# Summing the modulation's partial results over the partitions: one-column fp32 matmuls in place of transposes and a reduction

## The chip, the core and the metric

The kernel runs on one core of one Trainium2 chip. The metric is the device time in microseconds. Engines are named as in the profile: PE is TensorE's matmuls, PEld its weight loads, DVE is VectorE, ACT ScalarE, POOL GpSimd, SP the queue that issues the DMAs. A record is one instruction as the profiler saw it.

## What is computed

Two transformer blocks on 256 positions of 1024 features, one after the other. The first is modulated: a vector c gives shifts, scales and gates for its norms and residuals, and these come from one large product of a single row with a matrix.

```python
c_act = jax.nn.silu(c)                               # 1 x 1024
mod = c_act @ w_ada[l] + b_ada[l]                    # 1024 x 6144
sh1, sc1, g1, sh2, sc2, g2 = jnp.split(mod, N_MOD, axis=-1)
h = modulate(rms_norm(x, norm1_w[l]), sh1, sc1)      # h * (1 + scale) + shift
mix = hybrid_mixer(h, ...)                           # gated delta rule + short convolution
x = x + g1[:, None, :] * mix
h = modulate(rms_norm(x, norm2_w[l]), sh2, sc2)
x = x + g2[:, None, :] * swiglu(h, w_ffn_in[l], w_ffn_out[l])
shf, scf = jnp.split(c_act @ w_ada_f + b_ada_f, 2, axis=-1)   # 1024 x 2048
return modulate(rms_norm(x, normf_w), shf, scf)
```

The second block (attention with a relative bias, and a gated feed-forward part with a convolution) takes no modulation.

## The kernel before

All activations lie transposed, features on the partitions and the 256 positions along the free axis. Weights stream through three raw buffers of 128 x 2048 fp32 (1 MB a transfer). Each half of a raw buffer is a unit: ACT copies it to a rounded fp32r half (`wh`, L1454), DVE takes the rest (`wl`, L1841), and PE multiplies in three products: high weights by high activations, low by high (both L1093), high by low (L1099). Five pairs of `wh`/`wl` go round. The whole program is one list of events, `plan`, written by a simulated schedule in Python: a product's tile calls `tick()`, which moves every waiting task one step. Each engine then goes through `plan` in its order and issues its own part of each event; semaphores tie them together. So the order on every engine is fixed when the program is built.

The modulation's matrix, `ada`, has 16 blocks of 512 output columns, each in two transfers (kp 0 and 1). For a block, DVE multiplies 8 slices of 128 rows by the matching column of silu(c) and adds them in `accs` (128 x 512; `dve_ada`, L1737 and L1740). Each partition then holds a partial sum of all 512 columns, and these are still to be summed over the 128 partitions and laid out as 4 columns of 128 in `modc`. That is `ada_reduce` (L481): it waits six ticks (`LATER`), takes one of the two `misc` PSUM banks, lets PE work (event "red", 0: L1252), and two ticks later lets DVE work (event "red", 1: `dve_reduce`, L1746). Block 0 and the first half of block 1 go another way: PE multiplies the raw rows itself (L1232), ACT copies the resulting row (L1474), and four matmuls turn it into columns (L1241), to which DVE adds the bias (L1869). Block 1's own partial sum is added onto that.

What depends on it: `accs` has two buffers, and the next user waits for PE's "red"; a `misc` bank is free again after DVE's "red"; `mod_scale` (L1821), the scales of the norm and the residuals wait for "mod". Blocks 2, 3 and 1 are reduced in start-up, before and between the norm's first scales; their last use leads to the first product. Sixteen matmuls of `ones` by `eye` (L1249) stand before block 3's group and ten (L1084) before the first product; their results are not used. Blocks 8 and 9, 4 and 5, 6 and 7 come with the products gb, z and scout, and 10 to 15 with the first feed-forward part.

Of the kernel before, what the change touches and what calls it, by code (L numbers as in the profile page):

```python
# [8 lines left out]
ALU = mybir.AluOpType  # L9
# [167 lines left out]
MM = dict(stop=True, skip_group_check=True)  # L177
# [7 lines left out]
def _program(nc, a, out, ctx):  # L185
    def sb(name, shape, dt=F32, where=ctx):
        return where.enter_context(nc.sbuf_tensor(name, shape, dt))

    def signal(name, step=1):
# [12 lines left out]
    v_lo, v_ev, v_misc, v_gdn, v_att, v_norm = (signal("dve_" + n) for n in ("lo", "ev", "misc", "gdn", "att", "norm"))  # L202
# [4 lines left out]
    psum = [ctx.enter_context(nc.psum_tensor(f"ps{i}", [128, 512], F32)) for i in range(BANKS)]  # L207
# [10 lines left out]
    w1c = sb("w1c", [128, 8])  # L218
    w1n = sb("w1n", [128, 8])
    shn = sb("shn", [128, 8])  # L220
    adr = sb("adr", [128, 4])
    silc = sb("silc", [128, 8])
    R = sb("R", [128, T])
    accs = [sb(f"acc{i}", [128, 512]) for i in range(2)]
# [32 lines left out]
        bank=psum[8 - STREAMS + i]) for i in range(STREAMS)]  # L257
# [37 lines left out]
    eye = cst[:, CST["eye"]:CST["eye"] + 128]  # L295
    ones = cst[:, CST["ones"]:CST["ones"] + 128]
# [98 lines left out]
    def emit(*event):  # L395
        plan.append(event)
        made.add(event[0] if len(event) == 1 else event[0:3])
# [53 lines left out]
        while ("lo", u) not in made:  # L451
            low_before(cursor["lo"] + 1)

    rows_bank, reduced = [], []
    sums = {}

    def ada(i):
# [23 lines left out]
    def ada_reduce(b, slot):  # L481
        for _ in range(LATER):
            yield
        while b == 1 and ("turn", 1, 1) not in made:
            yield
        bank, before = yield from take(misc)
        emit("red", b, 0, slot, bank, before)
        acc.give(slot, p_misc, "red", b)
        yield
        yield  # L490
        emit("red", b, 1, slot, bank, reduced[-1] if reduced else None)
        reduced.append(b)
        misc.give(bank, v_misc, "red", b)

    def mod(b):
# [719 lines left out]
    def tensor_engine(e):  # L1215
        for ev in plan:
# [7 lines left out]
            elif kind == "ada_rows":  # L1224
                _, i, b, before = ev
# [4 lines left out]
                for n in range(4):  # L1230
                    kt = 4 * kp + n
                    ins = e.matmul(psum[b][0:1, :], silc[:, kt:kt + 1], raw[i % RAW][:, 512 * n:512 * n + 512],  # L1232
                                   start=kt == 0, **MM)
                ins.then_inc(*p_misc.up("rows", i))
            elif kind == "turn" and ev[2] == 1:
                _, blk, _, s, b, before = ev
                free(e, before)
                a_misc.wait_ge(e, "row", blk)
                d_cst.wait_ge(e, "cst")
                for n in range(4):  # L1240
                    ins = e.matmul(psum[b][:, n:n + 1], accs[s][0:1, 128 * n:128 * n + 128], ones[0:1, 0:1], start=True,  # L1241
                                   **MM)
                ins.then_inc(*p_misc.up("turn", blk))
            elif kind == "red" and ev[2] == 0:
                _, blk, _, s, b, before = ev
                free(e, before)
                if blk == 3:
                    for _ in range(16):
                        e.matmul(psum[b][:, 0:128], ones, eye, start=True, **MM)  # L1249
                v_misc.wait_ge(e, "ada", summed[blk][-1])  # L1250
                for n in range(4):
                    ins = e.transpose(psum[b][:, 128 * n:128 * n + 128], accs[s][:, 128 * n:128 * n + 128], eye)  # L1252
                ins.then_inc(*p_misc.up("red", blk))
            elif kind == "norm_sq":
                _, n, j, s, _, b, before = ev
                free(e, before)
                d_cst.wait_ge(e, "cst")
                a_norm.wait_ge(e, "sq", n, j)
                e.matmul(psum[b][:, 0:T], ones, sqs[s][:, 0:T], start=j == 0, **MM)
                e.matmul(psum[b][:, 0:T], ones, sqs[s][:, T:2 * T], start=False, **MM).then_inc(*p_norm.up("sq", n, j))  # L1260
            elif kind == "norm_col":
                b = ev[2]
                free(e, ev[3])
                a_norm.wait_ge(e, "r", N3)
                for t in range(2):
                    ins = e.matmul(psum[b][:, t:t + 1], R3[0:1, cs[t]], ones[0:1, 0:1], start=True, **MM)
                ins.then_inc(*p_norm.up("col"))
            elif kind == "norm_sum":
                _, n, s, b, before = ev
                free(e, before)  # L1270
                g_norm.wait_ge(e, "part", n, 3)
                e.matmul(psum[b][:, 0:T], ones, sqs[s][:, 0:T], start=True, **MM).then_inc(*p_norm.up("sum", n))
            elif kind == "close":
                _, n, _, s, _, s0, b, before, b2, before2 = ev
                free(e, before)
                g_norm.wait_ge(e, "part", n, 2)
                e.matmul(psum[b][:, 0:T], ones, sqs[s0][:, 0:T], start=True, **MM).then_inc(*p_norm.up("part", n))
                a_norm.wait_ge(e, "sq", n, 6)
                e.matmul(psum[b][:, 0:T], ones, sqs[s][:, 0:T], start=False, **MM)
                a_norm.wait_ge(e, "sq", n, 7)  # L1280
                e.matmul(psum[b][:, 0:T], ones, sqs[s][:, T:2 * T], start=False, **MM).then_inc(*p_norm.up("sum", n))
                warm(e, n, b2, before2)
            elif kind == "decays" and ev[1] == 3:
                b = ev[3]
                free(e, ev[4])
                v_misc.wait_ge(e, "G40")
                a_misc.wait_ge(e, "beta")
                for c in range(2):
                    e.transpose(psum[b][:, 64 * c:64 * c + 40], G40[0:40, cs[c]], eye[0:40, 0:40])
                e.matmul(psum[b][:, 128:136], G40[0:8, 127:128].to_broadcast([8, 128]), eye[0:8, 0:8], start=True,  # L1290
                         **MM).then_inc(*p_misc.up("G"))
            elif kind == "vturn":
                _, j, _, m, b, before = ev
                free(e, before)
                a_misc.wait_ge(e, "silu_v", j)
                for n in range(4):
                    ins = e.transpose(psum[b][:, 128 * n:128 * n + 128], tmps[m][:, 128 * n:128 * n + 128], eye)
                ins.then_inc(*p_misc.up("vturn", j))
            elif kind == "l2sum":
                _, j, n, s, b, before = ev  # L1300
                free(e, before)
                a_misc.wait_ge(e, "sq", j, n)
                e.matmul(psum[b][:, :], ones, sqs[s][:, :], start=True, **MM).then_inc(*p_misc.up("l2sum", j, n))  # L1303
            elif kind == "bias":
                b = ev[3]
                free(e, ev[4])
                d_dc.wait_ge(e, "dc")
                e.matmul(psum[b][0:16, 0:384], vec[0:32, VEC["rel"]:VEC["rel"] + 16], DC[:, 0:384], start=True,
                         **MM).then_inc(*p_misc.up("bias"))
# [433 lines left out]
            else:  # L1743
                ins.then_inc(*v_misc.up("ada", i))

    def dve_reduce(e, b, bank, previous):  # L1746
        col = modc[:, 4 * b:4 * b + 4]
        bias = col if b == 1 else v("b_ada", 4 * b, 4) if b < 12 else v("b_ada_f", 4 * (b - 12), 4)
        p_misc.wait_ge(e, "red", b)
        if previous is not None:  # L1750
            v_misc.wait_ge(e, "mod", previous)
        e.tensor_reduce(adr[:, :], psum[bank][:, :].rearrange("p (a b) -> p a b", a=4), mybir.AxisListType.X,
                        ALU.add).then_inc(*v_misc.up("red", b))
        v_misc.wait_ge(e, "red", b)
        if b == 1:
            v_misc.wait_ge(e, "turn", 1)
        e.tensor_tensor(col, adr[:, :], bias, ALU.add).then_inc(*v_misc.up("mod", b))

    def dve_scale(e, n, j, m, before):
        a_norm.wait_ge(e, "r", N2 if n == N3 else n)  # L1760
# [71 lines left out]
    def vector_engine(e):  # L1832
        for ev in plan:
            kind = ev[0]
            if kind == "lo":
                u = ev[1]
                un = units[u]
                i, n, c = un["item"]["i"], un["n"], un["c"]
# [26 lines left out]
            elif kind == "turn" and ev[2] == 1:  # L1865
                _, blk, _, s, b, _ = ev
                p_misc.wait_ge(e, "turn", blk)
                d_vec.wait_ge(e, "vec")
                ins = e.tensor_tensor(modc[:, 4 * blk:4 * blk + 4], psum[b][:, 0:4], v("b_ada", 4 * blk, 4), ALU.add)  # L1869
# [1 line left out]
                if blk == 0:  # L1871
                    v_misc.at[("turn", 0)] = v_misc.at[("mod", 0)]
            elif kind == "red" and ev[2] == 1:
                dve_reduce(e, ev[1], ev[4], ev[5])
            elif kind == "residual":
                _, n, j, pn = ev
                p = products[pn]
                b = psum[p["banks"][0]]
# [14 lines left out]
            elif kind == "close":  # L1893
                n, p = ev[1], products[ev[2]]
                for i in range(2):
                    kt, b = 6 + i, psum[p["banks"][i]]
# [9 lines left out]
            elif kind == "l2":  # L1906
                _, j, n, s = ev
# [3 lines left out]
            elif kind == "decays":  # L1911
                k = ev[1]
                if k == 0:
                    p = products[ev[3]]
# [16 lines left out]
                elif k == 4:  # L1931
                    b = psum[ev[3]]
# [17 lines left out]
            elif kind == "normed":  # L1950
                p = products[ev[1]]
# [9 lines left out]
            elif kind == "scx":  # L1961
                p, m = products[ev[1]], ev[3]
# [61 lines left out]
            elif kind == "bias":  # L2024
                b = ev[3]
# [153 lines left out]
```

## Time and profile before

| | |
|---|---|
| time, median of 3 runs | 913.32 us (912.99 to 917.46) |
| profiled execution | 921.88 us |
| its span, first to last instruction | 920.1 us |
| mean granted TensorE clock | 0.993 |
| instructions | 18632 |
| PE busy | 893.8 us (97%) |
| DVE busy | 667.6 us (73%) |
| ACT busy | 505.1 us (55%) |
| POOL busy | 65.8 us (7%) |

Busy time is the sum of an engine's records. Matmuls are pipelined, so the time that one occupies is read from the distance between the starts of successive records and not from its own duration, which is more than twice that. The chain that ended last is followed back from the last instruction, at each step to what released it.

### The profile page before, as it was taken

How to read it: one execution, taken by the hardware profiler on the slowest of the kernel's cores; microseconds unless marked ns; L12 is line 12 of the kernel's file. 1: busy time of each engine (PE TensorE's matmuls, PEld its weight loads, DVE VectorE, ACT ScalarE, POOL GpSimd, SP SyncE). 2: the span in 40 equal slices, each digit the busy share in tenths (PEclk: the TensorE clock that was granted, in tenths of full speed). 3: DMA queues.
4: the chain of work that ended last, by engine and by line, in shares of the span. 5: the costliest groups of instructions: out<-in, count | busy, mean ns of one | idle time of the engine just before them, and what ended most of it. 6: DMA issues, size and time to landing. Idle time of an engine off the chain costs nothing.

```text
span 920.1 us, 18632 instructions
## 1 busy us (share of the span) xinstructions
PE 893.8 (97%) x8020; PEld 850.1 (92%) x8020; DVE 667.6 (73%) x1132; ACT 505.1 (55%) x814; POOL 65.8 (7%) x83
## 2 busy tenths in 40 slices
PE   5998999999999999999999999999999999999997
PEld 2798998999898999999999999999899999999997
DVE  4878767566978677677798775588665688778652
ACT  2489667454354627555354444466665576666442
POOL 0100201021001001020000000120000200000011
PEclk9999999999999999999999999999999999999999
DMA  8754233333767665465988889526331455555631
GB/s 335 279 191 162 102 129 104 128 138 109 259 232 247 209 229 179 165 217 179 288 326 295 287 287 255 218 96 226 138 138 53 177 184 192 190 192 178 223 126 46
DMA packets 27681, 177.31 MB, mean 193 GB/s; under 512 B 2864, under 2 KB 5680, under 8 KB 7504
## 3 DMA queue, kind: packets, MB, share of 16 engines
q1 hardware_dynamic: 27600, 176.13, 54.7%
q8 instruction: 63, 1.03, 0.4%
q14 instruction: 18, 0.15, 0.0%
HBM read 174.29 MB, written 1.84 MB: 191 GB/s over the span
## 4 chain that ended last, share of the span: by engine, by line
PE 82%; DVE 8%; ACT 6%; DMA 2%; issue 1%; DVEq 0%; SPq 0%; ACTq 0%
PE ps L1093 46%; PE ps L1099 22%; PE ps L1091 2%; DVE wl L1841 2%; DVE acc L1740 1%; ACT wh L1454 1%; PE ps L1138 1%; PE ps L1146 1%; PE ps L1232 1%; PE ps L1149 1%; PE ps L1097 1%; DMA raw<-in_ada_dram 1%; PE ps L1252 1%; PE ps L1303 1%; DMA raw<-in_w_sc_dram 1%
## 5 line engine op out<-in xcount | busy, mean ns | idle before, releaser
L1093 PE MATMUL ps<-HH,wh 128*128 128x256 f32 x1480 | 374.1, 288 | 0.7 <-DVE wl L1841 0.2
L1841 DVE TENSOR_TENSOR wl<-raw,wh 128x1024 fp32r<-128x1024 f32 x265 | 320.2, 1228 | 73.4 <-ACT wh L1454 72.8
L1093 PE MATMUL ps<-HH,wl 128*128 128x256 f32 x1480 | 361.0, 279 | 0.0
L1454 ACT ACTIVATE wh<-raw 128x1024 fp32r<-128x1024 f32 x265 | 273.8, 1043 | 142.5 <-PE ps L1099 112.9
L1093 PEld LDWEIGHTS ps<-HH,wh 128*128 128x128 f32 x1480 | 280.4, 189 | 9.8 <-issue 4.3
L1093 PEld LDWEIGHTS ps<-HH,wl 128*128 128x128 f32 x1480 | 279.8, 189 | 1.9 <-issue 1.9
L1099 PE MATMUL ps<-HL,wh 128*128 128x256 f32 x1480 | 229.1, 279 | 0.3 <-DVE HL L1786 0.3
L1099 PEld LDWEIGHTS ps<-HL,wh 128*128 128x128 f32 x1480 | 197.1, 189 | 0.6 <-DVE HL L1786 0.5
L1093 PE MATMUL ps<-FH,wh 128*128 128x256 f32 x352 | 85.9, 278 | 0.0
L1093 PE MATMUL ps<-FH,wl 128*128 128x256 f32 x352 | 85.9, 278 | 0.0
L1740 DVE SCALAR_TENSOR_TENSOR acc<-raw,silc,acc 128x512 f32<-128x512 f32 x101 | 76.3, 756 | 8.0 <-DMA raw<-in_ada_dram 4.9
L1093 PEld LDWEIGHTS ps<-FH,wh 128*128 128x128 f32 x352 | 66.5, 189 | 0.0
L1093 PEld LDWEIGHTS ps<-FH,wl 128*128 128x128 f32 x352 | 66.3, 188 | 0.0
L1723 DVE SCALAR_TENSOR_TENSOR tmp<-ps,vec,tmp 128x255 f32<-128x255 f32 (+2 forms) x112 | 46.0, 474 | 27.5 <-ACT tmp L1522 25.8
L1099 PE MATMUL ps<-FL,wh 128*128 128x256 f32 x352 | 56.3, 279 | 0.0
L2073 POOL TENSOR_TENSOR sq<-sq 128x256 f32<-128x256 f32 x16 | 15.1, 943 | 515.4 <-ACT sq L1496 515.2
L1099 PEld LDWEIGHTS ps<-FL,wh 128*128 128x128 f32 x352 | 47.6, 188 | 0.0
L1613 ACT ACTIVATE FH<-tmp 128x512 fp32r<-128x512 f32 x22 | 14.0, 635 | 57.5 <-DVE tmp L2009 29.9
L1093 PE MATMUL ps<-YH,wh 128*128 128x256 f32 x128 | 32.6, 290 | 0.0
L1093 PE MATMUL ps<-YH,wl 128*128 128x256 f32 x128 | 31.3, 280 | 0.0
L1522 ACT ACTIVATE tmp<-ps,vec 128x256 f32<-128x256 f32 x44 | 22.3, 556 | 7.7 <-PE ps L1099 7.7
L1093 PEld LDWEIGHTS ps<-YH,wh 128*128 128x128 f32 x128 | 24.4, 191 | 0.5
(269 smaller groups left out, 1080.9 us busy)
## 6 DMA issues: line engine op xcount, KB each, us to landing
raw<-in_ada_dram SPq DMA_DIRECT2D x32, 1024.0 KB, 5.2
raw<-in_w_fi_dram SPq DMA_DIRECT2D x22, 1024.0 KB, 4.9
raw<-in_w_up_dram SPq DMA_DIRECT2D x22, 1024.0 KB, 4.8
raw<-in_w_rest_dram SPq DMA_DIRECT2D x20, 1024.0 KB, 4.8
raw<-in_w_in_dram SPq DMA_DIRECT2D x16, 1024.0 KB, 4.8
raw<-in_w_qkv_dram SPq DMA_DIRECT2D x12, 1024.0 KB, 4.8
raw<-in_w_o_dram SPq DMA_DIRECT2D x8, 1024.0 KB, 4.8
raw<-in_w_fo_dram SPq DMA_DIRECT2D x8, 1024.0 KB, 5.0
```

Of the source, the lines that this page charges most:

```text
L1091: e.matmul(o, x_hi[:, k0 + k, 128 * t:128 * t + 128], w[:, k, :], start=first and n + k == 0, **MM)
L1093: e.matmul(o, w[:, k, 128 * t:128 * t + 128], x_hi[:, k0 + k, :], start=first and n + k == 0, **MM)
L1097: ins = e.matmul(o, x_lo[:, k0 + k, 128 * t:128 * t + 128], wh[:, k, :], start=False, **MM)
L1099: ins = e.matmul(o, wh[:, k, 128 * t:128 * t + 128], x_lo[:, k0 + k, :], start=False, **MM)
L1138: ins = e.matmul(bank[g, 64 * c:64 * c + 64], S[f"d{n % 2}"][g, c, :], xz[g, 0, c, :], start=True, **MM)
L1454: e.activation(whl[u % HALF][0][:, 0:n], raw[i % RAW][:, c:c + n], ACT.Copy).then_inc(*a_hi.up(u))
L1522: e.activation(tmps[m][:, T * t:T * t + T], b[:, T * t:T * t + T], ACT.Identity, scale=v("conv2", 88 + ft), bias=v("conv2_b", ft)).then_in ...
L1613: e.activation(flat(dst, j), tmps[m][:, :], ACT.Copy).then_inc(*a_ev.up("hi", src, j))
L1723: e.scalar_tensor_tensor(out=cv, in0=b[:, T * t:T * t + T - s], scalar=tap, in1=cv, op0=ALU.mult, op1=ALU.add).then_inc(*v_ev.up("conv", n ...
L1740: ins = e.scalar_tensor_tensor(out=acc_, in0=w, scalar=c, in1=acc_, op0=ALU.mult, op1=ALU.add)
L1841: e.tensor_tensor(wl[:, 0:n], raw[i % RAW][:, c:c + n], wh[:, 0:n].bitcast(F32), ALU.subtract).then_inc(*v_lo.up(u))
L2073: e.tensor_tensor(sqs[s][:, 0:T], sqs[s][:, 0:T], sqs[s][:, T:2 * T], ALU.add).then_inc(*g_norm.up(*(("sum", n, j) if j else ("part", n, 0))))
```

## The change

The four transposes of a block's partial sums become four matmuls that have the same partial sums as weights and one column of ones as the streamed operand: each gives 128 sums over the partitions, in one column of PSUM. DVE then adds the bias straight from the four PSUM columns; the reduction and its small buffer `adr` go (a buffer of the same size keeps the layout of the memory). The plan, its order, the banks and the DMAs stay. "red" of DVE is now the same event as "mod".

```diff
@@ -218,7 +218,7 @@
-    adr = sb("adr", [128, 4])
+    sb("home_s", [128, 4])
@@ -488,8 +488,7 @@
-        emit("red", b, 1, slot, bank, reduced[-1] if reduced else None)
-        reduced.append(b)
+        emit("red", b, 1, slot, bank)
@@ -1249,7 +1248,7 @@
                 v_misc.wait_ge(e, "ada", summed[blk][-1])
                 for n in range(4):
-                    ins = e.transpose(psum[b][:, 128 * n:128 * n + 128], accs[s][:, 128 * n:128 * n + 128], eye)
+                    ins = e.matmul(psum[b][:, n:n + 1], accs[s][:, 128 * n:128 * n + 128], ones[:, 0:1], start=True, **MM)
                 ins.then_inc(*p_misc.up("red", blk))
@@ -1743,18 +1742,14 @@
-    def dve_reduce(e, b, bank, previous):
+    def dve_reduce(e, b, bank):
         col = modc[:, 4 * b:4 * b + 4]
         bias = col if b == 1 else v("b_ada", 4 * b, 4) if b < 12 else v("b_ada_f", 4 * (b - 12), 4)
         p_misc.wait_ge(e, "red", b)
-        if previous is not None:
-            v_misc.wait_ge(e, "mod", previous)
-        e.tensor_reduce(adr[:, :], psum[bank][:, :].rearrange("p (a b) -> p a b", a=4), mybir.AxisListType.X,
-                        ALU.add).then_inc(*v_misc.up("red", b))
-        v_misc.wait_ge(e, "red", b)
         if b == 1:
             v_misc.wait_ge(e, "turn", 1)
-        e.tensor_tensor(col, adr[:, :], bias, ALU.add).then_inc(*v_misc.up("mod", b))
+        e.tensor_tensor(col, psum[bank][:, 0:4], bias, ALU.add).then_inc(*v_misc.up("mod", b))
+        v_misc.at[("red", b)] = v_misc.at[("mod", b)]
```

## Rows read from the trace of the kernel before

**Rows 1.** The page's engine table: busy us, share, instructions.
```profile
PE 893.8 (97%) x8020; PEld 850.1 (92%) x8020; DVE 667.6 (73%) x1132; ACT 505.1 (55%) x814; POOL 65.8 (7%) x83
```

**Rows 2.** The page's chain that ended last, shares by engine.
```profile
PE 82%; DVE 8%; ACT 6%; DMA 2%; issue 1%; DVEq 0%; SPq 0%; ACTq 0%
```

**Rows 3.** Windows: stretch, length, PE, PEld, DVE, ACT, POOL, clock, DMA share, GB/s.
```profile
250.00:300.00 50.00, 48.25 (x494) 45.27 (x493) 41.30 (x74) 23.71 (x47) 5.96 (x10) 1.00 0.71 248
300.00:345.00 45.00, 43.67 (x464) 41.35 (x463) 32.61 (x54) 21.27 (x32) 1.45 (x3) 0.96 0.62 215
480.00:545.00 65.00, 65.00 (x570) 65.00 (x569) 54.38 (x67) 30.86 (x36) 0.00 (x0) 1.00 0.82 289
```

**Rows 4.** Windows of L1252 alone: PE and PEld records.
```profile
0.00:36.00 36.00, 1.97 (x12) 1.26 (x12) 1.00 0.86 324
236.00:545.00 309.00, 7.36 (x48) 5.40 (x48) 0.99 0.70 241
```

**Rows 5.** Line 1752 on DVE: ns min/median/max, first and last start.
```profile
L1752 DVE TENSOR_REDUCE adr<-ps x15: 673/683/690, 24.5 to 544.6; 128x4 f32<-128x512 f32 x15
```

**Rows 6.** Timeline (start, us, engine, line): a block in the product stream.
```profile
272.40 0.60 PE L1252 MATMUL ps<-cst,acc 128*128 128x128 f32 x4
...
272.96 0.28 PE L1093 MATMUL ps<-HH,wl 128*128 128x256 f32 x1
```

**Rows 7.** Timeline: two fp32 matmuls in the product stream.
```profile
340.72 0.39 PE L1174 MATMUL ps<-lc,inv 128*128 128x128 f32 x2
340.94 0.39 PE L1168 MATMUL ps<-v,k 128*128 128x128 f32 x2
...
341.28 0.28 PE L1093 MATMUL ps<-YH,wl 128*128 128x256 f32 x1
```

**Rows 8.** Timeline: runs of fp32 passes, 128- and 64-column weight tiles.
```profile
414.78 2.17 PE L1212 MATMUL ps<-cst 128*128 128x128 f32 x18
...
314.90 0.68 PE L1138 MATMUL ps<-xz,d 64*64 64x64 f32 x16
```

**Rows 9.** Timeline: four fp32 matmuls that stream one column.
```profile
33.39 1.05 PE L1241 MATMUL ps<-cst,acc 1*128 1x1 f32 x8 [0.68 <-ACT acc L1474]
```

**Rows 10.** Timeline of start-up: blocks 2, 3 and 1 and what follows.
```profile
22.69 0.59 ACT L1474 ACTIVATE acc<-ps 1x512 f32<-1x512 f32 x1 [1.90 <-PE ps L1252]
...
28.15 3.84 PE L1249 MATMUL ps<-cst 128*128 128x128 f32 x32
...
32.06 0.66 PE L1252 MATMUL ps<-cst,acc 128*128 128x128 f32 x4
...
32.75 0.59 ACT L1474 ACTIVATE acc<-ps 1x512 f32<-1x512 f32 x1 [3.96 <-PE ps L1252]
...
34.68 0.15 DVE L1869 TENSOR_TENSOR modc<-ps,vec 128x4 f32<-128x4 f32 x1
...
34.89 0.66 PE L1252 MATMUL ps<-cst,acc 128*128 128x128 f32 x4 [0.45 <-DVE modc L1869]
...
36.46 0.16 DVE L1757 TENSOR_TENSOR modc<-adr,modc 128x4 f32<-128x4 f32 x1
...
37.80 0.19 PEld L1093 LDWEIGHTS ps<-HH,wh 128*128 128x128 f32 x1 [0.22 <-DVE wl L1841]
...
42.48 0.50 PE L1099 MATMUL ps<-HL,wh 128*128 128x256 f32 x2 [0.34 <-DVE HL L1786]
```

**Rows 11.** The chain in order of time: start, us, what.
```profile
281.80 0.61 DVE adr L1752
```

**Rows 12.** Timeline of PE: three waits in the middle.
```profile
282.16 0.71 PE L1119 MATMUL ps<-KT 128*128 128x128 f32 x4 [1.58 <-ACT qg L1355]
...
297.74 0.45 PE L1146 MATMUL ps<-y,xz 64*64 64x64 f32 x8 [0.17 <-ACT y L1368]
...
322.49 0.44 PE L1155 MATMUL ps<-xz,l 64*64 64x64 f32 x4 [1.32 <-DVE inv L1662]
```

**Rows 13.** Windows, columns as in rows 3: a stretch of lower clock.
```profile
324.00:327.50 3.50, 3.50 (x29) 3.16 (x28) 3.15 (x7) 1.06 (x1) 0.00 (x0) 0.51 0.59 234
```

More of the change, by code:

```diff
@@ L452, in low_of @@
             low_before(cursor["lo"] + 1)
-    rows_bank, reduced = [], []
+    rows_bank = []
     sums = {}
@@ L1873, in vector_engine @@
             elif kind == "red" and ev[2] == 1:
-                dve_reduce(e, ev[1], ev[4], ev[5])
+                dve_reduce(e, ev[1], ev[4])
             elif kind == "residual":
```

## The prediction

> **What bounds the kernel now.** First the page's engine table: the chip's TensorE (PE) is busy for 97% of the span [rows 1]. Busy is not the same as bound, so next the chain that ended last: 82% of the span is PE work, 8% VectorE (DVE), 6% ScalarE (ACT) [rows 2]. Then the stages in which the modulation runs. Between 480 and 545 us PE is busy 65.00 of 65 us; between 250 and 300 and between 300 and 345 us it is busy 48.25 of 50 and 43.67 of 45 us [rows 3]. So whatever a block adds to PE's stream there moves everything behind it, and DVE, at 41.30 of 50 and 54.38 of 65 us, has room. The windows cut to the edited line say where its blocks are: 12 transposes (3 blocks) before 36 us and 48 (12 blocks) between 236 and 545 us [rows 4]. These two groups need two sums. The first 36 us are another regime: there PE, ACT and DVE wait on each other in a chain.
>
> **The change, part by part.** *Removed on DVE:* 15 reductions of median 0.683 us [rows 5]; the 15 adds of the bias stay. That is 15 x 0.683 = 10.2 us less work for an engine that is busy 73% [rows 1]. It is worth something only where the chain runs through DVE.
>
> *Replaced on PE, in the stream.* Four transposes stand as four records. In one block they start at 272.40, the next product's second matmul starts at 272.96: 0.56 us [rows 6]. (I read to the second matmul because the start of the first one after a change of kind is out of step.) The new form is an fp32 matmul, which this trace records as two passes, each with its own weight load: the four matmuls of L1241 are eight records [rows 9]. Two fp32 matmuls of 128 columns, four records, in the same position occupy 340.72 to 341.28, again 0.56 us [rows 7]. So a pass costs what a transpose costs, and there are now two passes per matmul.
>
> Does the single streamed column make a pass cheaper? Two rows give the bounds of a pass. With 128 streamed columns, 18 passes of L1212 take 2.17 us with a last record of 0.275 (its neighbours' median), so (2.17 - 0.275)/17 = 0.111 us each [rows 8]. With one streamed column, L1241's eight take 1.05 us with a last record of about 0.245, so (1.05 - 0.245)/7 = 0.115, with a slower first gap in it [rows 9]. These two differ by a factor of 128 in what is streamed and agree in price; what they share is a weight tile of 128 columns. L1241 loads only one partition of weights and the new matmul loads 128, but L1212 loads 128 partitions at the same price. I take 0.112 us. The bound from below is the pass with a 64-column tile, which has neither that width nor that stream: 16 passes in 0.68 us, (0.68 - 0.23)/15 = 0.030 us [rows 8]; it is the further one, since the new weight tile is the 128-column one.
>
> The block's price on PE: four passes more than now, 4 x 0.112 = +0.45 us. For the 12 blocks from 236 to 545 us: +5.4 us.
>
> What of it is hidden? PE has three waits in that stretch with room in them. At 282.16 us it waits 1.58 us for ACT's qg [rows 12]; but that wait follows a DVE and ACT sequence that PE itself started, so it moves as a whole. The same holds at 322.49 us, where PE waits 1.32 us for DVE [rows 12], at the end of a sequence of table loads and gates on ACT that starts from PE. At 297.74 us PE waits 0.17 us for ACT's y [rows 12], on a branch that hangs on a weight transfer; here the extra PE time does fill the wait: -0.2. The one reduction that the chain shows in this stretch, 0.61 us at 281.80 [rows 11], opens that same branch (it sits before the split of the weights and the release of a raw buffer). Without it the branch comes 0.6 us earlier, but PE's own queue is then later by three blocks' +1.3, so PE is what is late next, and the 0.6 us buys nothing beyond these 0.2. From 345 us on no wait of PE follows a reduction. Middle: 5.4 - 0.2 = +5.2 us.
>
> *Start-up.* Here I walk the rows [rows 10]. In all three blocks PE's group grows by 0.45 us, and somebody waits for each. (a) Block 2 at 22.0 us: ACT's copy of block 0's row needs the accumulator that this group frees, so that copy (22.69 us), its four row matmuls and DVE's add come 0.45 us later; then the reduction's 0.7 us is gone, so the first scale comes about 0.27 earlier. PE, however, is held by that add: its next row matmuls and the 16 warm-up matmuls of L1249 (28.15 us, 3.84 us long) are 0.45 later. (b) Block 3 starts 32.06 now; L1249 had ended its last pass about 0.2 us earlier than needed, so it starts at 32.28 and, with eight passes at the 1.05 us of L1241's eight, ends at 33.33 instead of 32.72. ACT's copy (32.75) moves by +0.6, the row matmuls from 33.39 to 34.00, DVE's add from 34.68 to 35.07. (c) Block 1 waits for that add: 34.89 becomes 35.28, its eight passes end at 36.33, and DVE's last add ends near 36.52 instead of 36.62. Two reductions (0.7 each) are gone and DVE waits in their place. Result for DVE: 0.1 us earlier. PE's warm-up behind block 1 ends 0.65 us later (0.39 + 0.45, less the 0.2 us that PE waited for DVE's weights at 37.80), but at 42.48 us PE waits 0.34 us for DVE, and the chain then goes over a weight transfer and ACT, where PE has room. I take -0.1 us; ends: -0.5 (if only DVE's side counts) and +0.65 (if only PE's).
>
> Added waits: none in number. DVE's add now waits straight for PE's group. In the stream the group is done long before (block at 272.40, reduction of it at 281.80), so nothing queues behind it. In (c) the split of the first weights (L1841) and the second scale queue behind it, which is counted. No DMA is moved and no engine queue is reordered. Bank and accumulator: the bank is released 0.7 us earlier by DVE, and PE releases the accumulator 0.45 us later; outside start-up the next user is far behind.
>
> Sum: +5.2 - 0.1 = **+5.1 us**. The profiled execution took 921.88 us (span 920.1 and 1.8 around it) and would take 927.0. It is 0.9% above the median of the timed runs, 913.32 us; I carry the same +5.1 us over, as the span runs nearly throughout at full clock (mean 0.993): **918.4 us**, +0.56%.
>
> A rule that speaks against this sum: the Trainium skill, "TensorE: Matmul & The Clock Gate", section "Back-to-back issue gap", gives an isolated matmul a gap that goes with the streamed columns and is some 25 ns for 1 to 64 of them. By it eight one-column passes would take 0.2 us instead of the transposes' 0.45, and each block would gain 0.25 us. L1241's 0.115 us per one-column pass disagrees; the same page warns that the figure leaves out the weight load.
>
> **Rivals.** *The single column is cheap (not slower).* Mechanism: a pass costs what it streams, and the weight load hides behind the neighbouring product. Price: the lower bound 0.030 per pass, so 8 x 0.030 = 0.24 against 0.45, -0.2 us per block, -2.5 in the stream; start-up then gives back its reductions on the chain, about -1.4 (two of 0.7), less the waits of (a) that vanish; together -4: about 909.5 us. It decides from the point where a pass falls below half a transpose, 0.055 us. Against it: the agreement of rows 8 and 9. For it: L1241 has never been seen between two products. Chance 0.06.
>
> *The middle absorbs it.* The six blocks between 250 and 345 us lie where the chain changes between PE, DVE and a transfer. If it is DVE and the transfer that hold PE there (the waits of rows 12), the six cost nothing and the reduction at 281.80 counts: 6 x 0.45 - 0.2 = 2.5 us less, +2.6: 915.9 us. For it: those waits, and DVE's 41.30 of 50 us. Against it: PE's queue between the waits is unbroken. Chance 0.15.
>
> *A second half-speed stretch.* From 324 to 327.5 us the granted clock is 0.51 (1.2 of 2.4 GHz), after PE had stood still before 322.49 us [rows 13, 12]; 3.5 us at half speed lose about 1.7. If the shifted waits (282.16, for one, is as long as that) bring one more such stretch: +6.8, 920.1 us. Chance 0.08.
>
> *Nothing changes in what is issued* is ruled out by the diff: the kind of matmul differs.
>
> **How the numbers follow.** Forecast 0.71 (918.4, on its own 917.3 to 919.6: start-up's ends and 0.1 us around the hidden part); absorbed 0.15 (915.9); another half-speed stretch 0.08 (920.1); cheap column 0.06 (909.5). The range leaves out the last and little else: low 914.8 (the absorbed case less 1 us of scatter of a median), high 921.0 (the clock case plus 1). A difference of 0.5%, about what a measurement of this kernel can tell from no change, is 4.6 us; the forecast is only 0.5 us beyond it. Of its 0.71 I put 0.49 above the bound and 0.22 below it, since the runs of before scatter from 912.99 to 917.46. Slower 0.49 + 0.08 = 0.57; same 0.22 + 0.15 + 0.03 = 0.40; faster 0.03.
>
> **What would show it.** Right: the new line has 120 records where L1252 had 60; eight of them, between two products, span about 1.0 us to the second matmul behind them (0.56 now); no reduction on DVE; busy time of DVE down by 10 us with the span up by 5; DVE's last start-up add near 36.5; PE's wait at 297.74 gone. Wrong: passes well below 0.11 us apart (cheap column), or PE's waits between 280 and 325 us shorter by the 2 us and more that the blocks added (absorbed), or a window of clock 0.5 that was not there.

## The result and the profile after

The changed kernel is slower, and by more than forecast.

| | before | changed |
|---|---|---|
| time, median of 4 runs each | 913.15 us (911.15 to 917.46) | 928.23 us (921.48 to 930.95) |
| ratio | | 1.0148, interval 1.0081 to 1.0215 |
| profiled execution, span | 921.88, 920.1 us | 929.71, 927.6 us |
| mean granted clock in it | 0.993 | 0.994 |

Twelve more runs in each of two later sets gave 1.0078 (1.0053 to 1.0104; median 920.38) and 1.0094 (1.0059 to 1.0129; median 924.33). The best estimate, from all 28 runs of the changed kernel, mean 923.6 us, and 137 of the kernel before, mean 915.2, is +8.4 us, give or take 1.6. Three slow executions of the kernel before (924.47, 1454.62 and 4934.83 us) are left out here and in every mean below. Single executions of either kernel scatter over 10 us, and where that comes from is a large part of what follows.

The engine table of the changed kernel, then its chain, answer to [rows 1] and [rows 2].

```profile
PE 902.8 (97%) x8080; PEld 858.6 (93%) x8080; DVE 657.9 (71%) x1117; ACT 504.9 (54%) x814; POOL 65.5 (7%) x83
...
PE 85%; DVE 6%; ACT 6%; DMA 2%; issue 1%; POOL 0%; SPq 0%; DVEq 0%; ACTq 0%
```

DVE has lost 9.7 us of work and the 15 reductions; PE has 60 records more. Of the chain that ended last, DVE's share fell from 8% to 6% and PE's rose from 82% to 85%: the chain has moved to PE.

The timeline of PE at the block that answers to [rows 6], then one among the feed-forward products.

```profile
273.49 0.95 PE L1251 MATMUL ps<-cst,acc 128*128 128x1 f32 x8
274.30 0.36 PE L1092 MATMUL ps<-HH,wh 128*128 128x256 f32 x1
274.50 0.28 PE L1092 MATMUL ps<-HH,wl 128*128 128x256 f32 x1
...
439.83 0.95 PE L1251 MATMUL ps<-cst,acc 128*128 128x1 f32 x8
440.64 0.36 PE L1092 MATMUL ps<-HH,wh 128*128 128x256 f32 x1
440.85 0.28 PE L1092 MATMUL ps<-HH,wl 128*128 128x256 f32 x1
```

A pass is one of the two records of an fp32 matmul. From the start of the eight passes to the second matmul behind them it is 1.01 us, where four transposes took 0.56: +0.45 us a block, as forecast. L1251's windows, against [rows 4], show the doubled records, and that all of them are in the same places:

```profile
0.00:40.00 40.00, 3.06 (x24) 2.91 (x24) 0.95 0.84 313
236.00:550.00 314.00, 11.70 (x96) 11.71 (x96) 1.00 0.68 237
```

**Where the 7.5 us between the two profiled spans lie.** I cut both traces at the first matmul of three products and take differences of their starts. Up to the first scout product (four stream blocks): +2.4 us, of which 4 x 0.45 = 1.8 are the blocks. From there to the first product with the feed-forward activations (eight blocks): +2.5, which is 8 x 0.45 = 3.6, less the half-clock stretch of [rows 13] that the changed execution did not have (1.7), plus 0.6. From there to attention, where nothing was changed at all: **+2.6**. Behind it 0. These two windows show 51 us of that third part, before and changed:

```profile
545.00:596.00 51.00, 51.00 (x452) 51.00 (x451) 28.36 (x30) 22.57 (x26) 5.69 (x5) 1.00 0.80 248
...
549.00:600.00 51.00, 51.00 (x436) 51.00 (x435) 27.29 (x29) 22.34 (x25) 5.71 (x5) 1.00 0.74 228
```

PE never waits in either, the clock is 1.00 in both, and the changed kernel gets 436 matmuls through where the other got 452. The starts of its products are 118 ns apart, those of the other 113. The page cannot show this: PE is busy 51.00 of 51 us both times.

**Start-up.** The chain in order of time (start, us, what), against [rows 10]:

```profile
26.10 4.96 PE ps L1231 x8
31.06 3.77 PE ps L1248 x32
34.83 0.80 PE ps L1251 x8
...
36.30 1.06 PE ps L1240 x8
...
37.60 1.07 PE ps L1251 x8
38.66 0.02 issue
38.69 0.16 DVE modc L1751
```

DVE's last add starts at 38.69, where the forecast let it end near 36.52. The eight row records of L1231 took 4.96 us; they took 3.59 before. The windows say why (columns as in [rows 3]):

```profile
25.50:28.80 3.30, 3.04 (x7) 0.72 (x7) 2.54 (x9) 1.84 (x5) 0.44 (x1) 0.50 0.94 380
29.00:39.00 10.00, 9.07 (x65) 7.16 (x64) 6.83 (x13) 3.09 (x5) 1.10 (x2) 1.00 0.76 269
39.20:42.40 3.20, 3.20 (x18) 3.20 (x17) 3.16 (x7) 1.76 (x5) 0.36 (x1) 0.50 0.43 182
```

The granted clock is 0.50 (1.2 of 2.4 GHz) in two stretches that ran at full clock before. From 26.1 us to block 1 the chain of start-up is now nearly all PE's: rows, warm-ups, block 3, rows turned, block 1. Before, it ran there over DVE's sums of the next blocks (L1740).

Little of this delay lasts, though. The first product (37.81 us before) starts 4.4 us later, the one at 88.1 us 2.1 later, and from the one at 113.0 us on 0.5 to 0.6. PE's waits before 88 us take up one part. The other is a half-clock stretch that both kernels have near 90 us, and that is 6.8 us long before and 3.4 us changed (windows, before and changed):

```profile
88.50:95.50 7.00, 7.00 (x31) 6.42 (x31) 6.62 (x17) 2.58 (x7) 0.94 (x2) 0.51 0.09 26
...
90.40:93.60 3.20, 3.20 (x15) 2.88 (x14) 2.67 (x8) 2.47 (x6) 0.94 (x2) 0.50 0.18 74
```

### The profile page after: what moved, and what is told of

The parts are those of the page before. It is cut to its first block, busy times and chain, and to the rows that moved or that the text cites. A ratio compares the mean times of both kernels' runs of the same rounds, so it can differ in the third digit from the quotient of the medians.

```text
span 927.6 us, 18740 instructions
## 1 busy us (share of the span) xinstructions
PE 902.8 (97%) x8080; PEld 858.6 (93%) x8080; DVE 657.9 (71%) x1117; ACT 504.9 (54%) x814; POOL 65.5 (7%) x83
## 4 chain that ended last, share of the span: by engine, by line
PE 85%; DVE 6%; ACT 6%; DMA 2%; issue 1%; POOL 0%; SPq 0%; DVEq 0%; ACTq 0%
PE ps L1092 46%; PE ps L1098 22%; PE ps L1090 2%; PE ps L1231 2%; DVE wl L1836 1%; PE ps L1251 1%; ACT wh L1453 1%; PE ps L1137 1%; PE ps L1145 1%; PE ps L1148 1%; PE ps L1096 1%; DMA raw<-in_ada_dram 1%; PE ps L1302 1%; DVE acc L1739 1%; DVE KT L1722 1%
## 5 line engine op out<-in xcount | busy, mean ns | idle before, releaser
L1655 DVE TENSOR_TENSOR xz<-xz,ps 128x256 f32<-128x256 f32 x32 | 13.0, 417 | 17.9 <-PE ps L1148 17.6
```

The costliest lines, as they stand in the source:

```text
L1655: e.tensor_tensor(xz4, xz4, b[:, 0:T], ALU.subtract).then_inc(*v_gdn.up("xz", h, n))
```

## The experiments

The theory after the first profile (A): the passes cost 5.4 us; the rest is the spacing that the product stream falls into behind a block, and something of start-up. The spacing is the distance between the starts of two matmuls that follow each other in a product. The rival (B): start-up, now a chain on PE with half-clock stretches, is the whole excess.

**start_only**

```diff
-  ins = e.transpose(psum[b][:, 128 * n:128 * n + 128], accs[s][:, 128 * n:128 * n + 128], eye)
+  if blk < 4:
+      ins = e.matmul(psum[b][:, n:n + 1], accs[s][:, 128 * n:128 * n + 128], ones[:, 0:1], start=True, **MM)
+  else:
+      ins = e.transpose(psum[b][:, 128 * n:128 * n + 128], accs[s][:, 128 * n:128 * n + 128], eye)
```

(and the bias added straight from PSUM for the same blocks)

> Only blocks 2, 3 and 1, the three of start-up, take the one-column fp32 matmuls; the twelve in the product stream keep transposes and reduction. Theory A (what a block costs in the product stream, plus the spacing that the stream of products settles into behind each block, 113 or 118 ns a matmul): within 2 us of before. Theory B (start-up: in the changed kernel the last start-up block came 2.6 us later, with a granted clock of 0.5 from 25.5 to 28.9 us, and that delay is the excess over the forecast): slower by 5 us or more.

Measured 1.0019 (0.9994 to 1.0043); median 917.95 against 914.76. Against both theories as written, the 12 times fall into two groups: five of 912.2 to 914.0 with mean granted clocks of 0.994 to 0.998, and seven of 917.7 to 920.7 with 0.989 to 0.992. The mean is +1.7 us. So start-up is not the whole excess (B); that it is not nothing this run alone does not show, as the interval holds 1. Its profiled execution, of 914.04 us, has one stretch of half clock in start-up and yet stands beside the five shorter times, so one such stretch does not make the longer ones:

```profile
37.30:40.50 3.20, 3.20 (x17) 3.20 (x16) 3.16 (x8) 2.49 (x7) 1.12 (x1) 0.50 0.34 141
```

**stream_only** (the same edit with `blk > 3`)

> Only the twelve blocks in the product stream are changed. Theory A: as the changed kernel, +8 to +15 us, of which 5.4 are the passes and the rest more time at the 118 ns spacing. Theory B: +5 us, the passes alone. Theory C (passes alone count, and the spacing is drawn anew by each execution with no bias): +5 us in the mean, scattering by some 5.

Measured 1.0064 (1.004 to 1.0087): median 920.63, mean 920.95 against 914.84 of the kernel before on that chip, +6.1 us. All eight runs lie between 919.3 and 923.8, mean clocks 0.993 to 1.0. Below A's +8 and a little above the +5 of B and C: the passes and perhaps a little more (the interval is 3.7 to 8.0 us).

**twice** (the kernel before, its reductions kept)

```diff
+  if blk > 3:
+      for n in range(4):
+          e.transpose(psum[b][:, 128 * n:128 * n + 128], accs[s][:, 128 * n:128 * n + 128], eye)
   for n in range(4):
       ins = e.transpose(psum[b][:, 128 * n:128 * n + 128], accs[s][:, 128 * n:128 * n + 128], eye)
```

> The kernel before with the four transposes of each of the twelve stream blocks issued twice: the same +0.45 us of PE per block as the change, the reductions kept, no fp32 passes in these blocks. If only PE's time per block counts: +5.4 us. If the kind of matmul (fp32 passes against transposes) decides into which spacing the products fall: +5.4 with a share of the 118 ns spacing as before (0.52), while stream_only has more (0.63 in the changed kernel).

Measured 1.0041 (1.0023 to 1.0058), mean +4.0 us, where +5.4 was expected. PE's time per block is indeed nearly the same as the change's, 0.99 to 1.00 us to the second matmul behind the group (its timeline of PE; the first matmul after the group starts out of step):

```profile
437.54 0.60 PE L1253 MATMUL ps<-cst,acc 128*128 128x128 f32 x4
437.98 0.60 PE L1255 MATMUL ps<-cst,acc 128*128 128x128 f32 x4
438.34 0.37 PE L1093 MATMUL ps<-HH,wh 128*128 128x256 f32 x1
```

With the reductions kept it is 2 us cheaper than stream_only without them. So taking 12 reductions off DVE bought nothing that shows in the stream, and eight passes are, if anything, worse neighbours than eight transposes.

**after_again**

> The changed kernel once more, on the same chip as the others. Theory A: equal to stream_only within 2 us. Theory B: above stream_only by 5 or more. Its profile shows whether the spacing behind each block is the same as in the first one (fixed by the code) or drawn anew.

Measured 1.0078 (1.0053 to 1.0104), 0.8 us above stream_only by the mean: A rather than B. In this profile the 60 us behind the last block run at 113 ns and the last 200 too, unlike in the first one: the spacing is not fixed by the code.

**before_again** (the kernel before against itself)

> The kernel before against itself: no difference, and a second profile of it. Every theory expects 0 within 2 us. What is asked is which spacing (113 or 118 ns a matmul) its long last products fall into, and how often it has half-clock stretches before 90 us: if as often as start_only, the start-up change has no part in the two groups of times that start_only shows (912 to 914 and 918 to 921).

Measured 0.999 (0.9958 to 1.0022). Its profiled execution, the one of 1454.62 us, had a mean granted clock of 0.56, so the second profile that was wanted was still missing.

**start_warm** (start_only, with three unused matmuls before each of the groups that turn a row into columns)

```diff
+  for _ in range(3):
+      e.matmul(psum[b][:, 0:128], ones, eye, start=True, **MM)
   a_misc.wait_ge(e, "row", blk)
```

> start_only plus three unused 128-column fp32 matmuls on PE before each of the two row-turning groups, where PE waits for ACT anyway (0.67 us of passes each into waits of 0.9). Theory A (start-up has become so thin in streamed work that PE's clock is halved for a stretch in about half of the executions, +6 us): the slow group of times goes or gets rarer; median 912.5 to 914, 1 to 2 us below before. Theory B (the slow group comes from later delays of the chain): stays as start_only, two groups, median near 918.

Measured 1.001 (0.998 to 1.004), mean +1.5 us over the kernel before; the median, 916.28, lies between the two expected. Five of 12 runs have a mean clock of 0.993 or less, and the profiled one has a half-clock stretch in start-up still, from 38.5 us. Filling these waits did not remove it. The five, at 917.3 us in the mean, are hardly slower than the other seven, at 916.9.

**start_wide** (against start_only)

```diff
-  ins = e.matmul(psum[b][:, n:n + 1], accs[s][:, 128 * n:128 * n + 128], ones[:, 0:1], start=True, **MM)
+  ins = e.matmul(psum[b][:, 128 * n:128 * n + 128], accs[s][:, 128 * n:128 * n + 128], ones, start=True, **MM)
```

> start_only with 128 streamed columns of ones in place of one, in the three start-up blocks: as many passes at the same 0.112 us, the same sums in every column, DVE takes one of each 128. If the single column, which leaves the array idle in most of a pass, brings the half-clock stretches: the slow group goes, median 912.5 to 914. If the longer group and the shifted waits bring them: as start_only, half of the executions at 918 to 921.

Measured 1.0028 (0.9995 to 1.0061), mean +2.4 us; three of 12 at a clock of 0.993 or less. Neither run supports its idea of what brings the half-clock stretches; with 12 runs each, 7, 5 and 3 of 12 can't be told apart. Its profiled execution is one of the long ones, 921.09 us, and has no half-clock stretch before 88 us; it is long by its last 200 us, which took 7 us more than start_only's.

**stream_half** (it leaves out the sums of half of the columns)

```diff
-  for n in range(4):
+  for n in range(2 if blk > 3 else 4):
       if blk > 3:
-          ins = e.matmul(psum[b][:, n:n + 1], accs[s][:, 128 * n:128 * n + 128], ones[:, 0:1], start=True, **MM)
+          ins = e.matmul(psum[b][:, 2 * n:2 * n + 2], accs[s][:, 128 * n:128 * n + 128], ones[:, 0:2], start=True, **MM)
```

> stream_only with two of a block's four fp32 matmuls, each streaming two columns: four passes per block, as many as the transposes of before; the sums of half of the columns are left out, and their places get copies. If the number of passes is the price: within 1.5 us of before (-5.5 against stream_only). If a change of kind in the stream costs by itself, or the spacing behind an fp32 group is worse: +1 to +6 us remain. If DVE's removed reductions were worth something in the stream: below before.

Measured 1.0029 (1.0 to 1.0059), mean +3.5 us: outside the 1.5 us that the number of passes alone would give. The timeline of PE prices the block all the same, 0.56 us for four passes with two streamed columns:

```profile
436.77 0.50 PE L1253 MATMUL ps<-cst,acc 128*128 128x2 f32 x4
437.13 0.36 PE L1093 MATMUL ps<-HH,wh 128*128 128x256 f32 x1
437.33 0.28 PE L1093 MATMUL ps<-HH,wl 128*128 128x256 f32 x1
```

The block costs what it cost before, and yet the times are in two groups, 914.1 to 915.4 (four) and 920.3 to 923.0 (eight), ten of the twelve at clocks from 0.997 up. So there is a second two-valued thing beside the clock, of 6 us. The last 200 us show it, in the two profiles of the next runs.

**after_third and before_third** (the two kernels once more)

> The changed kernel once more, on another chip. Theory A (5.4 us of passes, plus 1 to 3 us of the slower spacing behind the one-column groups, start-up about nothing): +6 to +9 us in the ratio of the medians. If the +15 us of its first four runs is its true size: +12 or more.

> The kernel before against itself: 0 within 2 us, and an undisturbed second profile. Theory A: behind its transposes that are entered at the fast spacing (113 ns) about half stay fast; its last products (from 705 us) may run at 113 ns, against 118 in the first profile, which by itself makes 6 us of difference between two executions of one kernel.

Measured 1.0094 (1.0059 to 1.0129) and 1.0 (0.9964 to 1.0036). The second profile of the kernel before has a span of 911.1 where the first had 920.1. These are windows of the last products, first profile and second:

```profile
701.00:900.00 199.00, 198.21 (x1673) 196.81 (x1673) 143.99 (x210) 115.44 (x163) 10.23 (x10) 1.00 0.48 170
...
701.00:900.00 199.00, 198.94 (x1744) 197.53 (x1743) 143.74 (x209) 116.33 (x166) 11.21 (x10) 1.00 0.48 170
```

One kernel, full clock in both, 1673 and 1744 matmuls in 199 us. From the first matmul of the attention's output product to PE's last record the first took 220.8 us and the second 213.2: 7.6 of the 9 us between the spans. The 11 undisturbed profiles up to here all took either 213 to 214 or 220 to 221 us for this part.

Both new profiles have the 113 ns spacing there, so they are a fairer pair than the first: 919.6 against 911.1, +8.5 us. Of it 5.4 are the passes and 0.5 is left of start-up (where the changed kernel again has three half-clock stretches). Another 1.2 are a wait that the kernel before does not have, 3.4 us behind a block, for weights whose transfer came late:

```profile
467.14 0.35 PE L1092 MATMUL ps<-HH,wh 128*128 128x256 f32 x1 [0.94 <-DVE wl L1836]
```

after_again lost 0.9 us at the same matmul; in the first changed profile and in stream_only the wait is absent. Of the remaining 1.4 us of the pair 1.0 is spacing.

**probe_t and probe_8**

```diff
+  if first and part != "low" and p["kind"] in ("ug", "uv"):
+      for _ in range(4):
+          e.transpose(o[:, 0:128], eye, eye)                          # probe_t
+          e.matmul(o[:, 0:1], eye, ones[:, 0:1], start=True, **MM)    # probe_8
```

> The kernel before with four unused transposes ahead of each of the 22 products of the last up-projection. Price by the group: 22 x 0.45 = +9.9 us, and behind a group entered at the fast spacing about half stay fast, none stays slow: about a third of that stretch at 118 ns.

> The same with four unused one-column fp32 matmuls (eight passes) ahead of each of the 22 products. By the passes: 22 x 0.90 = +19.8 us, 9.9 above probe_t. Theory A on the spacing: every group turns fast into slow and slow into fast, so about half of the stretch runs at 118 ns, 1 us more. If a one-column pass were cheap (the rival of the prediction): +5 us or less.

Measured 1.0075 (1.0047 to 1.0102) and 1.0168 (1.0125 to 1.0211). Profile against before_third, for the same last part: 223.1 and 233.3 us against 213.2, so +9.9 and +20.1, which is 0.45 and 0.91 per group. The price per pass stands, and the rival of the cheap column (at most +5) is out. In the medians the distance to the kernel before is smaller (+7.6, +16.6). Likely that is because the kernel before sometimes falls into the 118 ns spacing there, and the probes' two profiles did so for only a few products: of the groups in their profiles that were entered at 113 ns, all but one were left at 113, after transposes and after one-column passes alike. So the expectation that each eight-pass group flips the spacing failed in this place.

**Four kernels with a quiet end.** Two of the probe's groups in the last up-projection, in the kernel before and three changed ones:

```diff
+  if first and part != "low" and p["kind"] == "ug" and p["j"] in (1, 2):
+      for _ in range(4):
+          e.transpose(o[:, 0:128], eye, eye)
```

> The kernel before with four unused transposes ahead of each of two products (ug 1 and 2) of the last up-projection, +0.9 us of PE. If such a group puts the products behind it back to 113 ns: the times above 917 us go, the median is 912.5 to 914.5 and the scatter is halved; it would then be faster than the kernel before by 0 to 2 us in the mean. If it does not: +0.9 us and the same two groups of times.

> start_only with the same two groups. Against tail_before: -0.1 by the forecast; +1.5 to +2 if half-clock stretches of start-up come in a larger share of its executions (mean granted clock 0.993 or less in about 5 of 12, 1 of 10 in tail_before).

> stream_only with the same two groups. Against tail_before: +5.2 by the forecast; +6 with 0.5 to 1 us of slower spacing behind the eight-pass groups before 610 us. Mean granted clock 0.993 or less in about 1 of 10.

> The changed kernel with the same two groups. Against tail_before: +5.5 if only the passes count (the forecast), +7 to +8.5 if start-up costs 1.5 to 2 and the spacing in the first feed-forward part 0.5 to 1. If the first four runs of the changed kernel (+15) were typical: +12 or more.

| kernel | runs | median, us | mean | mean less tail_before | clock 0.993 or less |
|---|---|---|---|---|---|
| tail_before | 12 | 914.62 | 915.2 | | 1 |
| tail_start | 12 | 915.95 | 916.6 | +1.5 (-0.4 to 3.3) | 5 |
| tail_stream | 6 | 923.00 | 922.9 | +7.7 (6.4 to 9.0) | 0 |
| tail_after | 6 | 921.38 | 922.0 | +6.8 (4.1 to 9.5) | 1 |

Ratios to the kernel before: 1.0007 (0.9981 to 1.0033), 1.0031 (1.0002 to 1.006), 1.0103 (1.0075 to 1.013), 1.0093 (1.0058 to 1.0128). tail_before is no faster than the kernel before, but its standard deviation is 1.7 us against 3.5 beside it: the two groups do quiet the end, for 0.9 us of PE. tail_start is as the second of its two expectations has it, in time and in clocks, though its interval also holds the -0.1 of the forecast. tail_after lies between +5.5 and +8.5 and rules out the +12. It is not above tail_stream, though it has the change in start-up too; the two intervals overlap. tail_stream is 1.7 us above what was expected, and its profile shows what it has more: 4.6 us more lost to the slow spacing before attention than tail_before's. Of one such 51 us, tail_before and tail_stream:

```profile
545.00:596.00 51.00, 51.00 (x452) 51.00 (x451) 26.92 (x27) 22.75 (x25) 5.70 (x5) 1.00 0.77 240
...
549.00:600.00 51.00, 51.00 (x436) 51.00 (x435) 27.22 (x29) 22.23 (x25) 5.71 (x5) 1.00 0.73 227
```

**What the profiles say together on the spacing.** Between 430 and 560 us I noted for each block whether the ten matmuls before it and the dozen behind it are 113 or 118 ns apart, in the undisturbed profiles but those of twice and stream_half. Four transposes (nine profiles): entered at 113, 18 were left at 118 and 16 at 113; entered at 118, all 20 were left at 113. Eight fp32 passes (six profiles): entered at 113, **22 of 22 were left at 118**; entered at 118, 12 of 14 were left at 113. So a group of transposes can leave the stream at its fast spacing and these never did. stream_half says that it is the kind and not the number or the length: its four fp32 passes were entered at 113 four times and left at 118 four times, while the eight transposes of twice were entered at 113 two times and left once at either. These cases are not independent draws: four of the six profiles run through the same sequence. Summed over the stream from the first scout product to attention, the time beyond 113.4 ns a matmul was 3.1 us in the mean of the nine and 4.9 in the mean of the six: +1.8 us. The nine run from 2.2 to 5.6 and the six from 3.0 to 7.1, so this difference is barely clear of its scatter.

**On the clock.** Of 82 executions of kernels with the changed start-up 31 had a mean granted clock of 0.993 or less; of 206 with the old one, 21. The mean clock of tail_start's runs is 0.9952 and of tail_before's 0.9968; by an estimate from these, half-clock stretches cost 0.0016 x 915 = 1.5 us more, which is the whole difference in time. So the edit in start-up brings the lost clock with it. Where those stretches lie is not shown: no execution of the changed start-up at 0.993 or less was profiled. The eight undisturbed profiles with the changed start-up and the nine with the old one show little of it: six of the eight and two of the nine have a half-clock stretch before 60 us, but four of the eight and six of the nine have one near 89 us. At the product that starts at 113.0 us in the first profile, the eight stand 0.9 us ahead of that profile in the mean, and the nine 0.8.

## Why the prediction was wrong

*The direction and the mechanism were right; the size was not.* 918.4 was forecast and 928.2 measured on those four runs, outside the range up to 921.0; in the two later sets the medians were 920.4, inside it, and 924.3. The steps that failed are the scatter, which the sum put at 1 us of a median, and two terms: nothing for the spacing of the products behind a block, and -0.1 us for start-up.

*The price per block: right.* +0.45 us forecast, 0.45 in the timelines, 0.45 and 0.91 per group in the probes. The reading that made it was that two rows 128-fold apart in streamed columns [rows 8, 9] agree in the price of a pass. stream_only's +6.1 us (3.7 to 8.0) leaves no room for the second rival, by which half of these blocks would cost nothing (+2.6 for the whole change).

*DVE's relief in the stream: right as far as the runs tell.* 9.7 us less work and nothing gained that shows; twice, which keeps the reductions, is not dearer than stream_only.

*The hidden part: right, and small.* The wait at 297.74 [rows 12] is gone (the same matmuls start without a wait at 299.62), and that at 322.49 is 1.10 us now instead of 1.32:

```profile
299.62 0.45 PE L1145 MATMUL ps<-y,xz 64*64 64x64 f32 x8
...
324.89 0.44 PE L1154 MATMUL ps<-xz,l 64*64 64x64 f32 x4 [1.10 <-DVE inv L1661]
```

*Start-up: -0.1 us holds at full clock only.* tail_start's profile has no half-clock stretch in start-up, and there the walk comes out: against the start of its row records DVE's last add stands 0.2 us earlier than before, and the first product 0.5 later. At the product of 113.0 us it is 0.2 us ahead of twice, which has no such stretch either. But its runs lost 1.5 us more to the clock, and the means of the four kernels with the changed start-up alone are +1.5 to +2.4 us, each with an interval that reaches to 0 or near it. I had one more half-clock stretch as a rival, but put it at the waits in the middle and at a chance of 0.08. What brings the lost clock about is not settled: neither filled waits nor 128 streamed columns took it away with certainty.

*The missing term: the spacing of the product stream.* The sum let a block cost its own time and nothing behind it. [rows 6] and [rows 7] both have the matmuls behind the group in them, but I read only to the second. Behind eight passes that were entered at 113 ns the stream came out at 118 each time between 430 and 560 us. That was +1.8 us in the mean of the profiles, barely clear of their scatter, and 2.6 in the very pair shown first, in a stretch where nothing was edited.

*The scatter: mis-sized, and the largest of the three for the number.* "1 us of scatter of a median" was taken from three runs. The last 200 us alone have two lengths 7 us apart, and four runs can fall to one side. The profile had shown it, as 921.88 against 913.32, and I explained that difference away as a constant to be carried over.

With what was measured the sum is 5.4 + 1.8 + 1.5 - 0.2 = 8.5 us, against +8.4 by the means of all runs. That it fits so well is luck: the last two terms before the -0.2 are known to a microsecond or two each. The pair of profiles with a fast end also gives +8.5, but by other parts: 5.4 of passes, 0.5 of start-up, 1.4 of mostly spacing and 1.2 of the late weights at 467.14 us, which the sum has not. The remaining 6 us of the first result are most likely the draw of four executions, since the later, larger sets do not have them. The profiled one of the four had the slow end of 221 us. *Right among the rivals:* none; the cheap column is refuted by the probes, the absorbed middle by stream_only.

## What to carry to other kernels

Price a small matmul by its passes and its weight tile, not by the columns it streams: an fp32 matmul that replaces a transpose doubled the passes here, and each cost as much with 1 column as with 128. Moving work from an engine that nobody waits for to the one that bounds the kernel loses, even if more is removed (0.68 us a block) than added (0.45). And before forecasting half a per cent, look at how one unchanged stretch differs between two executions: count matmuls per window, since a busy share of 100% hides 4%.

## What the hardware showed that was not expected

- The stream of 256-column fp32r matmuls ran at one of two steady spacings, 113.4 or about 117.7 ns, at a granted clock of 1.00 in both and with no wait of PE. It changed only within the dozen or two matmuls behind a place where other matmuls or a gap came between the products, or where weights and activations changed roles (as at 639.30 us of the first profile). Within a run of products, once settled, it never did, in any undisturbed profile from 240 us on. In 199 us it is 1744 matmuls or 1673. What chooses is open; that the kind of matmul in between does not settle it alone is shown by the same eight passes leaving it at 118 in 22 of 22 cases in one stretch and at 113 in nearly all in another.
- Four unused transposes at two places of the last product stage went with half the scatter between executions (standard deviation 1.7 us in 12 against 3.5 in 23) without a gain in the median; by the price of a group they cost 0.9 us.
- An fp32 pass with a 128-column weight tile took 0.112 us with 1, 2 and 128 streamed columns and with 1 and 128 partitions of weights. Only the first gap of a group differs: behind a product the second thin pass starts 0.03 us after the first.
- The Trainium skill's figure of some 25 ns for isolated matmuls of 1 to 64 columns ("TensorE: Matmul & The Clock Gate", section "Back-to-back issue gap") did not show: the passes of one and two columns stood 0.112 us apart, but for the first two of a group. Its section "LDWEIGHTS (loading the stationary operand)", by which a load goes with the columns of the weight tile and not with its rows, fits the agreement of L1241 and L1251.
